# Joint norms between two products: sums gathered beside the first product, the gate factor put on y there, one pass over the tiles after it

## The chip, the cores and the metric

The kernel runs on one core of a Trainium2 chip. The metric is device time in microseconds (us), from the first to the last instruction of one execution; before the change the median of 3 runs is 2791.24 us (2790.05 to 2795.76). TensorE multiplies matrices, VectorE and ScalarE work elementwise, GpSimd too (slower), SyncE issues DMAs. In the profile they are PE (PEld for its weight loads), DVE, ACT, POOL and SP.

## The reference, cut to what matters

The program is a transformer-like block. Two places in it have the same form: a product's output y goes through a norm with gain and gate, is added to the residual x, and the sum goes through a second norm with its modulation into the next product.

```python
def rmsnorm(x, g):
    xf = x.astype(jnp.float32)
    y = xf * lax.rsqrt(jnp.mean(xf * xf, axis=-1, keepdims=True) + EPS)
    return (y * g.astype(jnp.float32)).astype(x.dtype)

def modulate(x, shift, scale):
    return x * (1 + scale) + shift

def half_ffn(h, shift, scale, gate, g_pre, g_post, w13, w2):
    u = modulate(rmsnorm(h, g_pre), shift, scale)
    return h + 0.5 * gate * rmsnorm(swiglu(u, w13, w2), g_post)

new_lat = h_lat + gt_l * rmsnorm(out_l, g_post)     # end of token_mixing
```

Place A: the first half_ffn's w2 product, then the norm in front of w_in. Place B: the token mixing's w_out product, then the norm in front of the second half_ffn. At A 768 tokens are worked on (512 of the sequence and 256 of the context), at B the 512.

## The kernel before, in words

Activations stand feature-major: 128 features on the partitions, tokens along the row, 8 tiles (KT) for 1024 features. So a norm over features sums over tiles and partitions; the sum over partitions is a matmul with a matrix of 1/1024 (mean_ones), which also spreads the mean over all partitions. Every product is done in three passes of fp32r (three_pass, L204 to L206): high part of the weight by high and low part of the data, low part of the weight by the high one. Weights come in slots of up to 128 x 2048 (STREAM): SyncE loads a slot (L169), GpSimd splits it into whi (L186) and wlo (L189) two slots ahead of TensorE, as soon as slot_done says that the buffer is free, and TensorE starts a slot when w_split and acc_free allow (pe_slot_begin). Slots at A: 8 of dn_a1, then gates (1), wk (4) and further ones in project_1. At B: 4 of w_out, then those of gu_b0.

In the last product VectorE adds each tile to y (L843) or copies it (L1833), ScalarE squares it (L526), VectorE adds the square to a running sum (L535). Behind the product stands NormFront: TensorE's mean of the sum (L588), square root on ScalarE in place in PSUM (L605), reciprocal on VectorE (L644) over all tokens; pass one makes y * gain * r and adds x (L637, L665) while ScalarE squares (L620) and TensorE sums (L596); a second root and reciprocal; pass two scales (L637), makes the high part on ScalarE (L628) and the low part on VectorE (L682). The first slot of the next product waits tile by tile for that low part (front.lo_ready); TensorE goes through the slots in order, gates first and then wk. The order of the work on each engine is the order of the code.

## Time and profile before

| | |
|---|---|
| median of 3 runs | 2791.24 us (2790.05 to 2795.76) |
| span of the profiled execution | 2793.2 us (its own time, 2.0 above the median) |
| TensorE busy | 2607.8 us, 93% |
| VectorE, ScalarE, GpSimd busy | 42%, 26%, 48% |

Busy time says what an engine was doing, not what the program waited for; the waits are read in the timelines, where an instruction row ends with the idle time in front of it and what released it. Times count from the span's start. GpSimd's splits of weights show when slots end, since each starts when TensorE has left its buffer.

### The profile page before, as it was taken

The numbers are of one execution on the slowest core, as the hardware profiler recorded it, in microseconds if no ns is written. First come the engines' busy times: TensorE is split into PE (matmuls) and PEld (weight loads), VectorE is DVE, ScalarE is ACT, GpSimd is POOL, SyncE is SP. The second block draws the span as 40 slices with busy tenths as digits, with TensorE's granted clock in tenths as the row PEclk, the third lists the DMA queues.
The fourth block names the chain that finished last, engine by engine and source line by source line (L and its number), as shares of the span: only waits on it lengthen the run. The fifth ranks groups of instructions, "written<-read, shape, count | busy, mean of one in ns | idle before, by whom it ended". The sixth has DMA issues, their size and how long they took to land. (4 is left out here: it accounts for less than half of the span.)

```text
span 2793.2 us, 35776 instructions
## 1 busy us (share of the span) xinstructions
PE 2607.8 (93%) x14270; PEld 2210.2 (79%) x14270; DVE 1172.2 (42%) x1682; ACT 715.5 (26%) x1152; POOL 1353.6 (48%) x431
## 2 busy tenths in 40 slices
PE   6999999995999899998999998999989999969997
PEld 4888888883889788876788886778887898867775
DVE  5112011227476464126310224455426225349997
ACT  5111000102220342101210113334432111126774
POOL 0443455451465035776477775566446777620000
PEclk8999999997999999999999998999999999988999
DMA  7443211112321003232123224220012232439994
GB/s 290 181 184 145 70 62 61 56 64 100 138 76 64 15 19 133 79 109 103 65 87 112 90 88 155 89 85 16 1 54 83 91 122 91 161 152 370 370 375 180
DMA packets 52444, 334.00 MB, mean 120 GB/s; under 512 B 6516, under 2 KB 7540, under 8 KB 19616
## 3 DMA queue, kind: packets, MB, share of 16 engines
q1 hardware_dynamic: 50736, 326.49, 31.5%
q0 software_dynamic: 1584, 5.78, 0.5%
q8 instruction: 87, 1.43, 0.2%
q14 instruction: 37, 0.30, 0.0%
HBM read 313.89 MB, written 22.07 MB: 120 GB/s over the span
## 5 line engine op out<-in xcount | busy, mean ns | idle before, releaser
L186 POOL TENSOR_TENSOR whi<-raw,one_col 128x2048 fp32r<-128x2048 f32 (+2 forms) x158 | 526.0, 3329 | 884.3 <-PE bank L206 782.0
L189 POOL TENSOR_TENSOR wlo<-raw,whi 128x2048 fp32r<-128x2048 f32 (+2 forms) x158 | 697.9, 4417 | 12.4
L204 PE MATMUL bank<-uh_a,whi 128*128 128x512 f32 (+1 forms) x704 | 239.2, 340 | 1.6 <-DVE ul_a L499 1.6
L205 PE MATMUL bank<-ul_a,whi 128*128 128x512 f32 (+1 forms) x704 | 237.5, 337 | 0.0
L206 PE MATMUL bank<-uh_a,wlo 128*128 128x512 f32 (+1 forms) x704 | 237.3, 337 | 0.0
L3383 DVE TENSOR_TENSOR moe_wl<-moe_raw,moe_wh 128x2048 fp32r<-128x2048 f32 x84 | 189.4, 2283 | 7.2 <-DMA xs_scratch<-moe_tok,moe_dest 5.4
L3319 ACT ACTIVATE moe_wh<-moe_raw 128x2048 fp32r<-128x2048 f32 x84 | 159.8, 1912 | 25.1 <-PE bank L3294 19.1
L204 PEld LDWEIGHTS bank<-uh_a,whi 128*128 128x128 f32 x704 | 134.1, 191 | 21.5 <-DVE ul_a L499 3.8
L206 PEld LDWEIGHTS bank<-uh_a,wlo 128*128 128x128 f32 x704 | 134.0, 190 | 14.2
L204 PE MATMUL bank<-uh_b,whi 128*128 128x512 f32 x352 | 138.1, 392 | 7.5 <-DVE ul_b L682 6.5
L205 PEld LDWEIGHTS bank<-ul_a,whi 128*128 128x128 f32 x704 | 134.2, 191 | 13.7
L205 PE MATMUL bank<-ul_b,whi 128*128 128x512 f32 x352 | 137.9, 392 | 0.0
L206 PE MATMUL bank<-uh_b,wlo 128*128 128x512 f32 x352 | 137.7, 391 | 0.0
L3231 POOL DMA_INDIRECT out_dram<-moe_y,moe_rows x7 | 6.7, 950 | 265.0 <-DVE moe_y L3440 265.0
L204 PE MATMUL bank<-fa_hh,whi 128*128 128x512 f32 (+1 forms) x352 | 118.7, 337 | 1.0 <-DVE fa_hl L822 1.0
L205 PE MATMUL bank<-fa_hl,whi 128*128 128x512 f32 (+1 forms) x352 | 118.5, 337 | 0.0
L206 PE MATMUL bank<-fa_hh,wlo 128*128 128x512 f32 (+1 forms) x352 | 118.3, 336 | 0.0
L785 ACT ACTIVATE fa_sil<-bank 128x512 f32<-128x512 f32 x22 | 13.2, 599 | 402.6 <-PE bank L206 402.6
L204 PE MATMUL bank<-xh_r,whi 128*128 128x512 f32 x256 | 100.5, 393 | 5.5 <-POOL wlo L189 3.3
L206 PE MATMUL bank<-xh_r,wlo 128*128 128x512 f32 x256 | 99.7, 389 | 0.0
L205 PE MATMUL bank<-xl_r,whi 128*128 128x512 f32 x256 | 99.6, 389 | 0.0
L3266 PE MATMUL bank<-moe_wh,moe_xsh 128*128 128x512 f32 x224 | 91.4, 408 | 2.9 <-DVE moe_xsl L3389 2.9
(547 smaller groups left out, 6350.0 us busy)
## 6 DMA issues: line engine op xcount, KB each, us to landing
moe_raw<-moe_w_dram SPq DMA_DIRECT2D x84, 1024.0 KB, 7.2
cond_ring<-w_ada_dram SPq DMA_DIRECT2D x27, 1024.0 KB, 6.7
raw<-gu_a_dram SPq DMA_DIRECT2D x22, 1024.0 KB, 5.0
raw<-gu_b_dram SPq DMA_DIRECT2D x22, 1024.0 KB, 4.9
raw<-wqkv_dram SPq DMA_DIRECT2D x12, 1024.0 KB, 4.7
raw<-dn_a_dram SPq DMA_DIRECT2D x16, 704.0 KB, 4.0
raw<-dn_b_dram SPq DMA_DIRECT2D x16, 704.0 KB, 4.0
n_ada<-w_ada_dram SPq DMA_DIRECT2D x9, 1024.0 KB, 19.6
```

The source lines that it names most:

```text
L186: e.nc.gpsimd.tensor_tensor(e.whi[p][:, 0:f], e.raw[p][:, 0:f], e.one_col[:, 0:1].to_broadcast([P, f]), ALU.mult).then_inc(e.w_hi, 1)
L189: e.nc.gpsimd.tensor_tensor(e.wlo[p][:, 0:f], e.raw[p][:, 0:f], e.whi[p][:, 0:f].bitcast(F32), ALU.subtract).then_inc(e.w_split, 1)
L204: e.nc.tensor.matmul(out, wh, xh, start=first, stop=False)
L205: e.nc.tensor.matmul(out, wh, xl, start=False, stop=False)
L206: return e.nc.tensor.matmul(out, wl, xh, start=False, stop=last)
L785: last = nc.scalar.activation(sil[p][:, 0:T], e.bank[2 * p][:, :], ACT.Silu)
L3231: nc.gpsimd.indirect_dma_start(out=e.dram["out"], out_offset=bass.IndirectOffsetOnAxis(ap=rows[r][:, :], axis=0), in_=Y[r][:, :], in_offse ...
L3266: nc.tensor.matmul(out, xsh[b % 2][:, k, :], w[:, cc], start=k == 0, stop=False)
L3319: nc.scalar.activation(wh[s % RING_W][:, :], raw[s % RING_RAW][:, :], ACT.Copy).then_inc(hi_done, 1)
L3383: nc.vector.tensor_tensor(wl[s % RING_W][:, :], raw[s % RING_RAW][:, :], wh[s % RING_W][:, :].bitcast(F32), ALU.subtract).then_inc(lo_done, 1)
```

## The change

NormSums gathers four sums while the product runs: of y squared, of z squared, of x times z and of x squared, where z is y with the gate factor. From the first comes r1, and as the mean of (x + r1 z) squared is xx + 2 r1 xz + r1 r1 zz, the second norm's factor r2 comes from all four without looking at x + r1 z. So the residual x is loaded before the last product and not behind it, ScalarE puts the gate factor on y (gate), and VectorE does five SBUF instructions per tile in the product's slots. For the last tile the gate is left to later, z squared and xz are made with the factor in the instruction. TensorE sums in four strips of tokens, each into 32 partitions of the bank, so that root and reciprocal see 192 or 128 columns instead of 768 or 512; matmuls with pick spread the rows again. JoinedNorm then makes one pass: z = y r1, y = z + x, t = y r2, u = t gs + shift on ScalarE, uh and ul. The first wk slot (at B the second gu_b0 slot) is split by ScalarE and VectorE and skipped by GpSimd. In project_1 first_pair takes gates and the first half of wk's first slot together, tile by tile, then wk's second half. The store of y goes out in eight parts, bias_tok behind it.

```diff
+class NormSums:
...
+    def act(self, act, k, written):
+        nc, r = self.e.nc, k % 2
+        if k == 0:
+            act.wait_ge(*self.x_in)
+        if k >= 2:
+            act.wait_ge(self.summed, max(1, k - 2))
+        nc.scalar.activation(self.tmp["xx"][r][:, :], self.x[:, k, 0:self.w], ACT.Square).then_inc(self.x_squared, 1)
+        if k == KT - 1:
+            nc.scalar.activation(self.e.warm[:, :], self.e.eps[:, 0:1], ACT.Sqrt).then_inc(self.gated, 1)
+        act.wait_ge(*written)
+        nc.scalar.activation(self.tmp["yy"][r][:, :], self.y[:, k, 0:self.w], ACT.Square).then_inc(self.y_squared, 1)
...
+        self.gate(k).then_inc(self.gated, 1)
+        act.wait_ge(self.gated, k + 1)
+        nc.scalar.activation(self.tmp["zz"][r][:, :], self.y[:, k, 0:self.w], ACT.Square).then_inc(self.z_squared, 1)
...
+    def pe(self, pe):
...
+        pe.wait_ge(self.summed, KT - 2)
+        for q in ("xx", "yy", "zz", "xz"):
+            for j in range(NSTRIP):
+                nc.tensor.matmul(self.out(q, j), e.mean_ones[:, 0:32], strips(self.acc[q][:, :])[:, :, 64 * j:64 * j + 64],
+                                 start=True, stop=False)
+        for q in ("xx", "yy", "zz", "xz"):
+            pe.wait_ge(ready[q], KT)
+            for j in range(NSTRIP):
+                last = nc.tensor.matmul(self.out(q, j), e.mean_ones[:, 0:32],
+                                        strips(self.tmp[q][1][:, :])[:, :, 64 * j:64 * j + 64], start=False, stop=True)
+            last.then_inc(self.sum_ready[q], 1)
...
+class JoinedNorm:
...
+    def act(self, act):
...
+        nc.scalar.activation(self.sd1[:, :], e.bank[self.sums.banks["yy"]][:, 0:q], ACT.Sqrt, bias=e.eps[:, 0:1]
+                             ).then_inc(self.sd1_ready, 1)
...
+        nc.scalar.activation(e.whi[p][:, :], e.raw[p][:, :], ACT.Copy).then_inc(e.w_hi, 1)
+        act.wait_ge(self.mean_ready, 1)
+        nc.scalar.activation(self.sd2[:, :], self.d[:, :], ACT.Sqrt, bias=e.eps[:, 0:1]).then_inc(self.sd2_ready, 1)
+        self.unpack(act, self.R1, self.r1, self.r1_psum, self.r1_ready)
...
+        self.unpack(act, self.R2, self.r2, self.r2_psum, self.r2_ready)
...
+    def dve(self, dve):
...
+        dve.wait_ge(self.sd1_ready, 1)
+        V.reciprocal(self.inv1[:, :], self.sd1[:, :]).then_inc(self.inv1_ready, 1)
...
+        link(V.tensor_tensor(self.a[:, :], bank["zz"], self.inv1[:, :], ALU.mult))
+        link(V.scalar_tensor_tensor(self.b[:, :], bank["xz"], 2.0, self.a[:, :], ALU.mult, ALU.add))
+        link(V.tensor_tensor(self.c[:, :], self.b[:, :], self.inv1[:, :], ALU.mult))
+        V.tensor_tensor(self.d[:, :], bank["xx"], self.c[:, :], ALU.add).then_inc(self.mean_ready, 1)
+        dve.wait_ge(self.sd2_ready, 1)
+        V.reciprocal(self.inv2[:, :], self.sd2[:, :]).then_inc(self.inv2_ready, 1)
+        dve.wait_ge(e.w_hi, self.g + 2)
+        V.tensor_tensor(e.wlo[p][:, :], e.raw[p][:, :], e.whi[p][:, :].bitcast(F32), ALU.subtract).then_inc(e.w_split, 1)
...
             feed_sp(e, sp, (fed, sp_span[1]))
             if late_load is not None:
-
-                sp.wait_ge(e.slot_done, START[f"{up}1"][1])
-                sp.dma_start(late_load[0][:, :, :], late_load[1]).then_inc(loaded, 16)
-                sp.wait_ge(loaded, 16)
+                sp.wait_ge(late_load[2], 16)
+                sp.wait_ge(sums.pick_in, 16)
...
-            feed_pool(e, pool, pool_span)
+            feed_pool(e, pool, (pool_span[0] + 1, pool_span[1]))
...
-            slots(pe, *START["gates"], fm(1, True, ready=lambda k: pe.wait_ge(front.lo_ready, k + 1)))
-            slots(pe, *START["wk"], fm(2, True))
+            def first_pair():
...
+                for k in range(KT):
+                    pe.wait_ge(front.lo_ready, k + 1)
+                    at = slice(k * P, (k + 1) * P)
+                    for p in (g % 2, 1 - g % 2):
+                        three_pass(e, e.bank[2 * p][:, :], e.whi[p][:, at], e.wlo[p][:, at], uh[:, k, 0:T], ul[:, k, 0:T],
+                                   k == 0, k == KT - 1)
+                        last = three_pass(e, e.bank[4 + p][:, 0:TC], e.whi[p][:, at], e.wlo[p][:, at], uh[:, k, T:W],
+                                          ul[:, k, T:W], k == 0, k == KT - 1)
+                        if k == KT - 1 and p == g % 2:
+                            last.then_inc(e.slot_done, 1)
```

Three places in the order of the instructions. First VectorE in w_out (place B), before; Y is the product's output, one slot is:

```order
L1833 COPY Y_6989<-bank 128x512
L1833 ISA
L1833 COPY Y_6989<-bank 128x512
L535 TENSOR_TENSOR w_out_run_acc<-w_out_run_acc,w_out_run_sq_6998 128x512 [waits w_out_run_summed,w_out_run_squared]
L530 REGISTER_ALU
L535 TENSOR_TENSOR w_out_run_acc<-w_out_run_acc,w_out_run_sq_6999 128x512 [waits w_out_run_summed,w_out_run_squared]
```

And now, VectorE in the second slot of w_out; XR is x, tmp and acc are NormSums' buffers:

```order
L2118 COPY Y_7318<-bank 128x512 [waits slot_done]
L2118 COPY Y_7318<-bank 128x512
L764 TENSOR_TENSOR s_tmp_xz_7335<-Y_7318,XR_7319 128x512 [waits s3_gated,s3_summed,acc_free]
L775 TENSOR_TENSOR s_acc_yy<-s_acc_yy,s_tmp_yy_7331 128x512 [waits s3_crossed,s3_summed,s3_z_squared,s3_x_squared]
L775 TENSOR_TENSOR s_acc_zz<-s_acc_zz,s_tmp_zz_7333 128x512
L775 TENSOR_TENSOR s_acc_xz<-s_acc_xz,s_tmp_xz_7335 128x512
L775 TENSOR_TENSOR s_acc_xx<-s_acc_xx,s_tmp_xx_7337 128x512
L764 TENSOR_TENSOR s_tmp_xz_7336<-Y_7318,XR_7319 128x512 [waits s3_gated,s3_summed,acc_free]
```

Four more additions follow, then the next slot's copies: ten instructions with two SBUF inputs where two stood. Second, VectorE behind dn_a1 (place A), a tile of pass two before:

```order
L637 SCALAR_TENSOR_TENSOR bank<-y_a,gs,bank 128x512 [waits n2_lo_ready]
L637 SCALAR_TENSOR_TENSOR bank<-y_a,gs,bank 128x256
L682 SCALAR_TENSOR_TENSOR ul_m<-bank,mods,uh_m 128x512 [waits n2_hi_ready]
L682 SCALAR_TENSOR_TENSOR ul_m<-bank,mods,uh_m 128x256
L637 SCALAR_TENSOR_TENSOR bank<-y_a,gs,bank 128x512 [waits n2_lo_ready]
```

And VectorE in the single pass now; n_r1s and n_r2s are the spread factors:

```order
L929 TENSOR_TENSOR y_a<-n_z_3649,xr 128x768 [waits n2_z_ready]
L918 TENSOR_TENSOR n_z_3650<-y_a,n_r1s 128x768 [waits n2_added]
L938 TENSOR_TENSOR n_t_3651<-y_a,n_r2s 128x768 [waits n2_u_ready,n2_added]
L922 TENSOR_TENSOR ul_m<-n_u_3654,uh_m 128x768 [waits n2_hi_ready]
L929 TENSOR_TENSOR y_a<-n_z_3650,xr 128x768 [waits n2_z_ready]
```

The additions of x that stood in pass one are now between the tiles of the only pass. Third, TensorE at the start of the gates slot, before (whi_51 and wlo_53 hold gates):

```order
L204 MATMUL bank<-uh_m,whi_51 128x512 [waits n2_lo_ready,acc_free,w_split]
L205 MATMUL bank<-ul_m,whi_51 128x512
L206 MATMUL bank<-uh_m,wlo_53 128x512
L204 MATMUL bank<-uh_m,whi_51 128x512 [waits n2_lo_ready]
L205 MATMUL bank<-ul_m,whi_51 128x512
```

And TensorE there now (whi_52 and wlo_54 hold wk's first slot):

```order
L204 MATMUL bank<-uh_m,whi_51 128x256
L205 MATMUL bank<-ul_m,whi_51 128x256
L206 MATMUL bank<-uh_m,wlo_53 128x256
L204 MATMUL bank<-uh_m,whi_52 128x512
L205 MATMUL bank<-ul_m,whi_52 128x512
L206 MATMUL bank<-uh_m,wlo_54 128x512
L204 MATMUL bank<-uh_m,whi_52 128x256
L205 MATMUL bank<-ul_m,whi_52 128x256
L206 MATMUL bank<-uh_m,wlo_54 128x256
L204 MATMUL bank<-uh_m,whi_51 128x512 [waits n2_lo_ready]
```

Between two waits for a tile stand twelve matmuls instead of three.

## Rows read from the trace of the kernel before

**Rows 1.** The page, busy time and share of the span by engine:
```profile
PE 2607.8 (93%) x14270; PEld 2210.2 (79%) x14270; DVE 1172.2 (42%) x1682; ACT 715.5 (26%) x1152; POOL 1353.6 (48%) x431
```

**Rows 2.** Busy time by stretches: us; PE, PEld, DVE, ACT, POOL busy; PEclk; DMA; GB/s:
```profile
637.20:680.00 42.80, 16.12 (x36) 7.55 (x36) 33.18 (x46) 13.02 (x18) 8.69 (x2) 0.74 0.23 91
680.00:700.20 20.20, 16.75 (x48) 11.21 (x49) 14.22 (x26) 6.31 (x12) 0.00 (x0) 0.53 0.23 69
1309.50:1339.20 29.70, 11.98 (x18) 3.91 (x19) 22.38 (x26) 10.11 (x15) 8.14 (x2) 0.74 0.17 63
```

**Rows 3.** Timeline of GpSimd, place A: start us, us, engine, line, operation, [idle before]:
```profile
700.48 3.60 POOL L186 TENSOR_TENSOR whi<-raw,one_col 128x2048 fp32r<-128x2048 f32 x1 [54.44 <-PE bank L206]
...
717.14 3.60 POOL L186 TENSOR_TENSOR whi<-raw,one_col 128x2048 fp32r<-128x2048 f32 x1 [8.38 <-PE bank L206]
```

**Rows 4.** Timeline of VectorE, place A:
```profile
616.45 1.25 DVE L535 TENSOR_TENSOR fa_run_acc<-fa_run_acc,fa_run_sq 128x768 f32<-128x768 f32 x1 [1.01 <-ACT fa_run_sq L526]
...
637.33 1.02 DVE L843 TENSOR_TENSOR y_a<-y_a,bank 128x512 f32 x2 [6.28 <-PE bank L206]
...
671.47 4.98 DVE L644 RECIPROCAL bank<-bank 128x512 f32<-128x512 f32 x2 [3.94 <-ACT bank L605]
...
692.12 2.35 DVE L682 SCALAR_TENSOR_TENSOR ul_m<-bank,mods,uh_m 128x512 fp32r<-128x512 f32 x4
```

**Rows 5.** Timeline of TensorE, place A:
```profile
641.74 2.93 PE L588 MATMUL bank<-fa_run_acc,mean_ones 128*128 128x512 f32 x4 [4.55 <-DVE fa_run_acc L535]
...
680.04 0.76 PE L204 MATMUL bank<-uh_m,whi 128*128 128x512 f32 x1 [9.66 <-DVE ul_m L682]
```

**Rows 6.** Timeline of VectorE and ScalarE: the first norm, then place A:
```profile
26.84 7.04 DVE L491 TENSOR_TENSOR n_x<-n_x,n_rstd 128x768 f32<-128x768 f32 x8
...
39.31 2.28 DVE L471 TENSOR_TENSOR wlo<-raw,whi 128x2048 fp32r<-128x2048 f32 x1
...
45.93 1.29 ACT L456 ACTIVATE n_t<-n_x,mods,gs 128x512 f32<-128x512 f32 x2
47.25 0.85 ACT L460 ACTIVATE uh_a<-n_t 128x768 fp32r<-128x768 f32 x1
...
690.02 1.05 ACT L628 ACTIVATE uh_m<-bank,mods 128x512 fp32r<-128x512 f32 x2 [1.18 <-DVE bank L637]
```

**Rows 7.** Timeline of TensorE in the conditioning step (two rows per matmul):
```profile
33.45 1.93 PE L280 MATMUL bank<-n_ada,cond_sc 128*32 128x256 f32 x16 [0.55 <-DMA n_ada<-w_ada_dram]
...
81.44 2.80 PE L280 MATMUL bank<-cond_ring,cond_sc 128*32 128x256 f32 x48
```

**Rows 8.** Groups of instructions by line and shape: busy us, mean ns, idle before:
```profile
L843 DVE TENSOR_TENSOR y_a<-y_a,bank 128x256 f32 x8 | 3.3, 414 | 0.0
```

**Rows 9.** Timeline of TensorE in the first slot of gu_b0:
```profile
1343.63 0.63 PE L205 MATMUL bank<-ul_b,whi 128*128 128x512 f32 x1
...
1344.34 0.40 PE L204 MATMUL bank<-uh_b,whi 128*128 128x512 f32 x1
1344.58 0.40 PE L205 MATMUL bank<-ul_b,whi 128*128 128x512 f32 x1
```

**Rows 10.** Timeline of GpSimd, place B:
```profile
1280.53 4.94 POOL L189 TENSOR_TENSOR wlo<-raw,whi 128x2048 fp32r<-128x2048 f32 x1
...
1320.99 4.54 POOL L189 TENSOR_TENSOR wlo<-raw,whi 128x2048 fp32r<-128x2048 f32 x1
1352.79 3.60 POOL L186 TENSOR_TENSOR whi<-raw,one_col 128x2048 fp32r<-128x2048 f32 x1 [27.26 <-PE bank L206]
```

**Rows 11.** DMA issues: name, queue, count, KB each, us to landing:
```profile
xr<-x_dram SPq DMA_DIRECT2D x1, 3072.0 KB, 11.7
```

**Rows 12.** Timeline of VectorE in w_out:
```profile
1279.38 6.64 DVE L535 TENSOR_TENSOR w_out_run_acc<-w_out_run_acc,w_out_run_sq 128x512 f32<-128x512 f32 x2 [0.80 <-ACT w_out_run_sq L526]
...
1309.58 1.29 DVE L1833 COPY Y<-bank 128x512 f32 x2 [1.74 <-PE bank L206]
1311.69 1.49 DVE L535 TENSOR_TENSOR w_out_run_acc<-w_out_run_acc,w_out_run_sq 128x512 f32<-128x512 f32 x2 [0.81 <-ACT w_out_run_sq L526]
```

More of the change, by code:

```diff
@@ L741, in _ @@
             pool.wait_ge(e.w_split, 2)
-            feed_pool(e, pool, pool_span)
+            feed_pool(e, pool, (pool_span[0] + (front is not None and cond is None), pool_span[1]))
         @block.tensor
@@ L773, in _ @@
                 slots(pe, d0 + 1, d1, down_slot)
+            if sums is not None:
+                sums.pe(pe)
         @block.scalar
@@ L800, in _ @@
                     slots(act, g0, g1, silu_slot)
-            slots(act, *START[f"{down}1"], lambda nm, i, p, g, ih, gh: running.act(act, tile_at(y, i), i, p, g))
+            if sums is None:
+                slots(act, *START[f"{down}1"], lambda nm, i, p, g, ih, gh: running.act(act, tile_at(y, i), i, p, g))
+            else:
+                slots(act, *START[f"{down}1"], lambda nm, i, p, g, ih, gh: sums.act(act, i, (e.acc_free, g + 1)),
+                      straight=True)
         @block.vector
@@ L846, in out_slot @@
                     last.then_inc(e.acc_free, 1)
-                    if half == 1:
+                    if half == 1 and sums is None:
                         running.dve(dve, yv, i, p, g)
-                slots(dve, *START[f"{down}{half}"], out_slot)
+                    elif half == 1:
+                        sums.dve(dve, i, (e.acc_free, g + 1))
+                slots(dve, *START[f"{down}{half}"], out_slot, straight=half == 1 and sums is not None)
     if front is not None:
@@ L999, in tm @@
                 return body
-            slots(pe, *START["gates"], fm(1, True, ready=lambda k: pe.wait_ge(front.lo_ready, k + 1)))
-            slots(pe, *START["wk"], fm(2, True))
+            def first_pair():
+                g = START["gates"][0]
+                pe_slot_begin(e, pe, g)
+                pe_slot_begin(e, pe, g + 1)
+                for k in range(KT):
+                    pe.wait_ge(front.lo_ready, k + 1)
[7 more added lines that the diff above has]
+                            last.then_inc(e.slot_done, 1)
+                p = 1 - g % 2
+                for out, c in ((e.bank[2 * p + 1][:, :], slice(0, T)), (e.bank[4 + p][:, TC:2 * TC], slice(T, W))):
+                    for k in range(KT):
+                        at = slice((KT + k) * P, (KT + k + 1) * P)
+                        last = three_pass(e, out, e.whi[p][:, at], e.wlo[p][:, at], uh[:, k, c], ul[:, k, c], k == 0,
+                                          k == KT - 1)
+                last.then_inc(e.slot_done, 1)
+            first_pair()
+            k0, k1 = START["wk"]
+            slots(pe, k0 + 1, k1, fm(2, True))
             slots(pe, *START["wq"], fm(2, False))
@@ L1015, in _ @@
             act.wait_ge(e.slot_done, g0 + 1)
-            act.wait_ge(front.stored, 16)
+            act.wait_ge(front.stored, 16 * KT)
             nc.scalar.activation(GR[:, 0:T], e.bank[2 * (g0 % 2)][:, :], ACT.Identity, bias=e.params[:, at:at + 1])
@@ L3541, in layout_inputs @@
     dram["strip_sel"] = strip
+    pick = np.zeros((P, NSTRIP, P), np.float32)
+    for m in range(NSTRIP):
+        pick[32 * m, m] = 1.0
+    dram["pick"] = pick.reshape(P, NSTRIP * P)
     def pair(name, wa, wb, w2, half_tiles):
@@ L3696, in program @@
                      product_gate(e, "w_four", 4, yfh, yfl, GF), mixed, out])
+        back_in.close()
     uh, ul = at("uh_b", [P, KT, T], 0, F32R), at("ul_b", [P, KT, T], 16384, F32R)
-    n3 = NormFront(e, "n3", T, Y1, uh, ul, "gu_b0", acc=acc, post=(1, XR), pre=2)
+    n3 = JoinedNorm(e, "n3", sums, uh, ul, 2, START["gu_b0"][0], MAIN + 123904, (e.bank[0],), (e.bank[1],), joint=False)
     Y2 = at("Y2", [P, KT, T], 107520)
```

247 lines of the change are left out of this document (229 added, 18 removed).

## The prediction

> **What bounds the kernel now.** I read first the engines' busy times: TensorE is busy for 93% of a span of 2793.2 us and no other engine, its own weight loads apart, for half of it [rows 1]. A change elsewhere can therefore pay only where TensorE waits, so next I took busy time by stretches around the two places that the diff touches [rows 2]. Place A lies between the last slot of dn_a1 and the first slots of project_1: in the 42.8 us after 637.2 us TensorE works for 16.1, and in the next 20.2 us, the gates slot, its clock is 0.53 of full. Place B lies between w_out and gu_b0: of 29.7 us it works for 12.0, on the norms' own sums. Both waits end with a chain of steps on VectorE and ScalarE.
>
> When a slot ends is best read on GpSimd, which splits the weights two slots ahead as soon as a slot is done. At A gates ends at 700.4 and the first wk slot, wk0, at 717.0 us [rows 3]; dn_a1 ended at 637.2, just before VectorE takes its last tile [rows 4]. My marker is the end of wk0. VectorE at A has two reciprocals of 5.0 us, each with a pass over the tiles behind it; the second pass runs from 676.5 to 694.5 [rows 4]. TensorE gets its first tile at 680.0 us [rows 5], and each of the others waits for its ul_m tile.
>
> **Place A, step by step.** From 637.2 us the last tile is added until 638.35 [rows 4]. ScalarE then squares y (0.85) and squares it again with the gate factor as scale, a pair like the one at 690.02 us, 1.05 us [rows 6]: 640.4. TensorE's sums are eight groups of four matmuls with 32 output rows, 192 columns each. The conditioning step has that shape: 24 matmuls, six groups of 256 columns, took 2.80 us at full clock, 0.47 a group, and two groups 1.93 at half clock [rows 7]. So 0.35 us a group; four fit before 640.4, and the last is done by 641.2. (If the four strips didn't overlap, the groups would cost four times that and A some 7 us more.) Then: square root of 192 columns 0.4 (640.9); reciprocal, 192 columns at 6.5 ns from 4.98 us for 768 [rows 4], 1.3 (642.2); four short dependent steps, each just below the 0.41 us of 256 columns [rows 8] with 0.1 for the semaphore, 1.9 (644.1); square root 0.4 and reciprocal 1.3 (645.9); on VectorE the low part of wk0, 2.28 [rows 6]: 648.3. Its high part, on ScalarE, lies beside the four steps. The spreading matmuls of R1 (768 fp32 columns, 2.93 us [rows 5]) and two unpackings of about 0.5 end before 648.3; those of R2 at about 650, and the first use is at 651.
>
> The pass has four instructions of 768 columns for each tile (z, add, t, low part), all with both inputs in SBUF. Eight such took 7.04 us back to back [rows 6], so 0.87 each, 3.5 us a tile. ScalarE needs 2.1 a tile for u and uh (1.29 and 0.85 [rows 6]) and stays under that. 32 instructions are 28 us; the first add waits for z (0.2) and the last low part for u and uh (about 1.7): 30 us, end at 678.3. The old passes end at 694.5 [rows 4]. So 16 us come from fewer and shorter reciprocals, from joint norms and from one pass.
>
> The other part is first_pair: for each tile TensorE now has gates and the first half of wk0, 12 matmuls, 2.1 us at full clock (0.23 for 512 columns [rows 9] and 0.12 for 256) and 3.8 at half. Of wk0's 16.6 us [rows 3] half has moved under the pass. After 678.3 come 2.1 us for the last tile and 8.3 for the second half: marker at 688.7 against 717.0, **28.3 us gained**. GpSimd's split for wk1 starts when gates is done, 679.4, and takes 3.60 + 4.6 [rows 3, 10]: 687.6, just in time. The cost of a low clock: before, TensorE spent most of the gates slot at half clock, with gaps, and at B, without gaps, it rose after 5 us, at 1344 [rows 2, 9]. Here it has 3.8 us of work per 3.5 at half clock, so it is as dense as at B. If it stays at half clock to the end, the second half costs 16.6 instead of 8.3, +8.
>
> What else moves at A costs nothing by my count. The x load (11.7 us [rows 11]) is issued at 545.4 in front of the load of dn_a1's fourth slot; that one is due on GpSimd at 568.5, 23 us later. The new sums put xz and four additions behind each dn_a1 slot: 1.0 + 5 x 0.87 on VectorE and about 3.6 on ScalarE. VectorE's two-input instructions wait while GpSimd runs (below, at B). So they start after the split, at about 6 us of an 11.46 us slot, and end at 10.7. That just fits, and the last sums are done at 635. The store in eight parts and the bias behind it are waited for by ScalarE's GR (at about 680); the fourth wk load has until 705.
>
> **Place B, where GpSimd's hold on the port that both share decides.** In w_out GpSimd splits 2048 columns (3.60 + 4.6 us) in each of three slots of 10.9 us, and the two additions of a slot took 6.64 us in the first (three such rows), but 1.49 once GpSimd stood still [rows 12]. One gets in between GpSimd's two instructions, the next waits for the end of the second; GpSimd itself waits at most one VectorE instruction (4.94 against 4.54 [rows 10]). New are ten of these per slot instead of two (six in the first). I walk through it with 0.61 us each, between 0.58 (the 0.87 by columns) and 0.75 (half of 1.49, where each waits for the one before): by the end of the second slot (1287.7) xz0, xz1 and two or three additions are done; GpSimd holds the port until 1291.9; one addition; the copy of slot two ends at 1293.9 (about 1289 before), TensorE needs it by 1298.6. In the third window xz2 and two additions by 1299.2, one more at 1302.8, then none until GpSimd is done at 1308. Free from there: six instructions (1311.9), the copy of slot three (1313.1), 1.6 for y squared and the gate on ScalarE, ten (1321.1), the last copy, 1.6, five: 1327.2. Without the lock it would be 1315.7; the old sum was done at 1313.2.
>
> Then at half clock (TensorE idle since 1309.5) eight groups of 0.45, 1330.8, and the block's end, 1331.2 (0.45 from the two groups in 1.93 [rows 7]). Square root, reciprocal (128 columns), four steps, root and reciprocal: 0.4 + 0.9 + 1.8 + 0.5 + 0.9 = 4.5, the low part 2.3: 1338.0. The pass at 512 columns: 0.61 x 4 = 2.4 a tile, 21 in all: 1359.1, and the last six matmuls 1.4: 1360.5. Before, this slot ended at 1352.7 [rows 10]. **7.8 us lost.**
>
> The page "SBUF — State Buffer" of the Trainium skill (Who interferes with whom) speaks against this part: a VectorE instruction with two SBUF inputs and a GpSimd instruction that reads SBUF exclude each other for a whole instruction. The trace agrees (6.64 against 1.49). By a shared bandwidth instead, the additions would only be slower, and B would come out between the two sums.
>
> The sum: 28.3 - 7.8 = 20.5 us, 2793.2 - 20.5 = 2772.7 for an execution like the profiled one. The runs' median, 2791.24, is 2.0 lower: **2770.7 us**. What follows is a sequence bound by TensorE, which moves as a whole; nothing there starts by another clock than the slots.
>
> **The rivals.**
> The lock bites less: VectorE slips in more often and GpSimd, which has 2.3 us of slack a slot, takes the delay. Up to 11.5 us come back at B, 2759. For it: GpSimd's 0.4 more [rows 10] shows that VectorE can pass it. Against: the second addition didn't pass in any of the three windows [rows 12]. 20%.
> Less at A: the clock stays at half behind the pass (+8), or the strips of the sums run in series (+7 at A, +8 at B): 2779 to 2786. For it: 0.53 over the whole gates slot before. Against: the six groups in 2.80 us, and the clock at B [rows 7, 9]. 20%.
> Slower: two-input instructions keep, without GpSimd, the 1.25 us that they show in dn_a1 [rows 4] instead of 0.87, at either width +0.38, on the 64 of both passes and on the 16 that stand alone at the end of w_out: 30 us, 2801. It decides from +0.26 each. Against it speak the 7.04 us for eight and the 1.49 for two; for it only that these rows come from a stage with another layout. 4%.
> The change doesn't do what it says, VectorE's pass is the bound and nothing is won by first_pair (TensorE waits for wk0's split or for a load): +10, 2781, 4%.
>
> **Numbers.** My case has 52%, 2766 to 2776. The range takes in the lock that doesn't bite (2759) with 2 below for its error, and half clock with serial strips at one place: 2757 to 2786. A measurement of this kernel tells 0.2%, 5.6 us, from no change. Faster by more than that, below 2785.6: 92%; within it 4%; slower 4%.
>
> **What would show it.** In the profile after: at A the first uh_m matmul at about 655, then one group of twelve every 3.5 us, the last low part at about 678, wk0's end near 689 (GpSimd's second split after dn_a1). At B the last addition of the sums near 1327 minus the 28 of A, with single additions of 3 to 5 us in w_out, and the first gu_b0 slot longer after w_out than the 43.3 us of before (1309.4 to 1352.7), by about 8. The prediction is wrong if a dn_a1 or w_out slot gets longer (GpSimd would then be the one that waits), if the pass takes over 4 us a tile, or if TensorE is at half clock after the pass.

## The result and the profile after

The changed kernel takes 2770.46 us (median of 4 runs, 2769.15 to 2774.13) against 2791.66 us of the kernel before in the same session (4 runs, 2790.05 to 2795.76): ratio 0.9926, 95% interval 0.9912 to 0.9940. Predicted were 2770.7 us and a range of 2757 to 2786. The profiled execution has a span of 2767.8 us, 25.4 less than the one before.

The page of the profile after, its first row: busy us, share and number of instructions.

```profile
PE 2587.4 (93%) x14376; PEld 2205.1 (80%) x14376; DVE 1205.0 (44%) x1705; ACT 760.8 (27%) x1217; POOL 1334.9 (48%) x427
```

TensorE's busy time is 20 us less than in [rows 1], though its work isn't less: busy time counts clock and stalls too. VectorE and ScalarE have more to do, and the time fell all the same, so totals don't explain it. The stretches do: busy time by stretches, from dn_a1's end to wk0's, in a slot of w_mproj (used below), and from w_out's end to the end of gu_b0's first slot. The columns are those of [rows 2].

```profile
635.90:686.54 50.64, 35.77 (x226) 29.06 (x227) 36.51 (x43) 25.34 (x39) 8.21 (x3) 0.90 0.37 135
...
1188.82:1200.22 11.40, 11.30 (x50) 9.32 (x51) 0.00 (x0) 0.00 (x0) 8.21 (x4) 1.00 0.45 142
...
1276.40:1325.98 49.58, 22.11 (x130) 16.50 (x131) 38.70 (x62) 25.94 (x38) 0.00 (x1) 0.69 0.11 40
```

From the last tile's addition to GpSimd's split behind wk0, A took 79.8 us before (637.33 to 717.14 [rows 3, 4]) and takes 50.6 now: 29.2 gained, 28.3 predicted. B took 43.3 before (from 1309.5, the end of w_out's first slot and three slots of 10.88, to 1352.79 [rows 10]) and takes 49.6: 6.3 lost, 7.8 predicted. Together 22.9. The other 2.5 us between the two spans stand in code that the change doesn't touch: after the change the first split of GpSimd comes 1.3 us earlier, and a slot of w_mproj took 12.98 us before at a clock of 0.87 and 11.40 after at 1.00; the remaining stretches come to 0.4 us the other way. The kernel of A alone (below), which has the same code up to there, has the first split at the old place again and 12.95 us in that slot. So these 2.5 us are differences between executions, and the medians, 21.2 apart, are nearer to the 22.9 than to the 25.4. How finely one execution tells two kernels apart, the traces of all eleven kernels show: the stretch from wk0's end to the end of w_out's first slot took 555.8 to 559.7 us and the stretch behind B 1440.0 to 1445.0, though the kernels do the same work there, while A is 50.6 us in all five kernels that share its code and B 49.5 to 49.6 in five. The intervals can therefore be compared to 0.1 us and whole executions only to a few us. The end of w_out's first slot in the kernel before:

```profile
1276.85 3.60 POOL L186 TENSOR_TENSOR whi<-raw,one_col 128x2048 fp32r<-128x2048 f32 x1 [2.60 <-PE bank L206]
```

GpSimd's splits after the change, the markers of both places (start, us, then the instruction and the idle time ahead of it):

```profile
677.16 3.60 POOL L186 TENSOR_TENSOR whi<-raw,one_col 128x2048 fp32r<-128x2048 f32 x1 [48.19 <-PE bank L206]
...
686.54 3.60 POOL L186 TENSOR_TENSOR whi<-raw,one_col 128x2048 fp32r<-128x2048 f32 x1 [1.10 <-PE bank L206]
...
1243.74 3.60 POOL L186 TENSOR_TENSOR whi<-raw,one_col 128x2048 fp32r<-128x2048 f32 x1 [2.59 <-PE bank L206]
...
1254.62 3.78 POOL L186 TENSOR_TENSOR whi<-raw,one_col 128x2048 fp32r<-128x2048 f32 x1 [2.27 <-PE bank L206]
...
1325.98 3.60 POOL L186 TENSOR_TENSOR whi<-raw,one_col 128x2048 fp32r<-128x2048 f32 x1 [51.42 <-PE bank L206]
```

VectorE at A (it answers to [rows 4]): the last tile, its xz, the first reciprocal, the start of the pass, and its last low part.

```profile
635.93 1.02 DVE L1105 TENSOR_TENSOR y_a<-y_a,bank 128x512 f32<-128x512 f32 x2 [2.38 <-PE bank L206]
636.99 1.15 DVE L760 SCALAR_TENSOR_TENSOR s_tmp_xz<-y_a,gg,xr 128x512 f32<-128x512 f32 x2
639.18 1.35 DVE L899 RECIPROCAL n_inv<-n_sd 128x192 f32<-128x192 f32 x1 [1.04 <-ACT n_sd L860]
...
646.04 0.94 DVE L918 TENSOR_TENSOR n_z<-y_a,n_r1s 128x768 f32<-128x768 f32 x1
647.02 0.96 DVE L929 TENSOR_TENSOR y_a<-n_z,xr 128x768 f32<-128x768 f32 x1
647.89 0.95 DVE L918 TENSOR_TENSOR n_z<-y_a,n_r1s 128x768 f32<-128x768 f32 x1
...
674.67 0.96 DVE L922 TENSOR_TENSOR ul_m<-n_u,uh_m 128x768 fp32r<-128x768 f32 x1 [1.38 <-ACT uh_m L885]
```

The whole chain from the last tile to the first z takes 10.1 us, as much as two reciprocals alone took before (5.0 each [rows 4]); two-input instructions of the pass follow each other by 0.87 us (647.02, 647.89), as the prediction took them.

TensorE at A (it answers to [rows 5]): the sums in strips (first, second and last group), the spreading of the first factor, and the first matmuls of two tiles.

```profile
635.82 0.53 PE L784 MATMUL bank<-s_acc_xx,mean_ones 128*32 128x192 f32 x8
636.17 0.51 PE L784 MATMUL bank<-s_acc_yy,mean_ones 128*32 128x192 f32 x8
...
639.24 0.51 PE L789 MATMUL bank<-s_tmp_xz,mean_ones 128*32 128x192 f32 x8
640.67 1.54 PE L830 MATMUL bank<-n_inv,s_pick 128*128 128x192 f32 x8 [0.93 <-DVE n_inv L899]
...
653.34 0.76 PE L204 MATMUL bank<-uh_m,whi 128*128 128x512 f32 x1 [7.74 <-DVE ul_m L922]
...
667.14 0.50 PE L204 MATMUL bank<-uh_m,whi 128*128 128x512 f32 x1 [1.12 <-DVE ul_m L922]
```

Groups of twelve matmuls start at 663.67, 667.14 and 670.62, 3.48 us apart, and each waits about 1.1 us for its low part: VectorE is the bound. The last two tiles come faster, since z has already been made for them (673.35 and 675.69, with waits of 0.4 and 0.0). The clock by stretches of the same place:

```profile
653.30:658.80 5.50, 5.46 (x16) 4.62 (x17) 5.50 (x7) 3.35 (x5) 0.00 (x0) 0.50 0.20 76
658.80:675.60 16.80, 13.11 (x69) 10.61 (x68) 15.38 (x18) 10.77 (x15) 0.00 (x0) 1.00 0.19 70
```

It is 0.50 for the first 5.5 us, in which TensorE has no gap, and 1.00 from then on, with TensorE at work for 78%.

VectorE in w_out and behind it, where the lock was predicted (it answers to [rows 12]):

```profile
1254.25 0.69 DVE L775 TENSOR_TENSOR s_acc_xz<-s_tmp_xz,s_tmp_xz 128x512 f32<-128x512 f32 x1
1254.85 4.09 DVE L775 TENSOR_TENSOR s_acc_xx<-s_tmp_xx,s_tmp_xx 128x512 f32<-128x512 f32 x1
...
1270.02 5.09 DVE L764 TENSOR_TENSOR s_tmp_xz<-Y,XR 128x512 f32<-128x512 f32 x1
...
1277.73 1.28 DVE L2118 COPY Y<-bank 128x512 f32<-128x512 f32 x2
...
1292.71 0.68 DVE L775 TENSOR_TENSOR s_acc_xx<-s_acc_xx,s_tmp_xx 128x512 f32<-128x512 f32 x1
1293.31 0.74 DVE L760 SCALAR_TENSOR_TENSOR s_tmp_xz<-Y,gg,XR 128x512 f32<-128x512 f32 x1
```

An addition or an xz takes 0.6 us where GpSimd stands still, 4.09 and 5.09 where it is at work: 1254.85 is held until GpSimd's high part (1254.62, 3.78) is done, and 1270.02 until the low part is (from 1269.62, 4.94). The copy of the third slot starts at 1277.73, 12.2 us after that slot's end, and the last addition of the sums ends at 1293.4, 17.0 us behind w_out.

### The profile page after: what moved, and what is told of

Its sections match the earlier page's. It is cut to its first block and busy times, and to the rows that moved or that the text cites. A ratio compares the mean times of both kernels' runs of the same rounds, so it can differ in the third digit from the quotient of the medians.

```text
span 2767.8 us, 36011 instructions
## 1 busy us (share of the span) xinstructions
PE 2587.4 (93%) x14376; PEld 2205.1 (80%) x14376; DVE 1205.0 (44%) x1705; ACT 760.8 (27%) x1217; POOL 1334.9 (48%) x427
## 5 line engine op out<-in xcount | busy, mean ns | idle before, releaser
L186 POOL TENSOR_TENSOR whi<-raw,one_col 128x2048 fp32r<-128x2048 f32 (+2 forms) x156 | 520.4, 3336 | 876.7 <-PE bank L206 782.6
L189 POOL TENSOR_TENSOR wlo<-raw,whi 128x2048 fp32r<-128x2048 f32 (+2 forms) x156 | 684.8, 4390 | 12.2
```

The costliest lines, as they stand in the source:

```text
L186: e.nc.gpsimd.tensor_tensor(e.whi[p][:, 0:f], e.raw[p][:, 0:f], e.one_col[:, 0:1].to_broadcast([P, f]), ALU.mult).then_inc(e.w_hi, 1)
L189: e.nc.gpsimd.tensor_tensor(e.wlo[p][:, 0:f], e.raw[p][:, 0:f], e.whi[p][:, 0:f].bitcast(F32), ALU.subtract).then_inc(e.w_split, 1)
```

## The experiments

Intervals are read as above: A from VectorE's last addition to y in dn_a1 to GpSimd's split behind wk0, B from w_out's end (its first slot's end and three slots of 10.88) to the end of gu_b0's first slot. Where GpSimd makes no split in w_out, its end is that of TensorE's last matmul, which in the changed kernel is 0.1 us earlier than the other reading. Before they are 79.8 and 43.3, after 50.6 and 49.6 us.

### w_out_split: GpSimd out of w_out

```diff
-            feed_pool(e, pool, pool_span)
+            feed_pool(e, pool, (pool_span[0], pool_span[1] - (3 if runs[-1].seg == "w_out" else 0)))
...
     def act_body(act, i, p, g):          # in product_out_sums
+        if i < 3:
+            act.wait_ge(e.w_landed[p], 16 * ((g + 2) // 2) + 16)
+            act.wait_ge(e.slot_done, g + 1)
+            act.wait_ge(e.w_split, g + 2)
+            e.nc.scalar.activation(e.whi[p][:, :], e.raw[p][:, :], ACT.Copy).then_inc(e.w_hi, 1)
...
         last.then_inc(e.acc_free, 1)     # in dve_body, behind the copies
+        if i < 3:
+            dve.wait_ge(e.w_hi, g + 3)
+            e.nc.vector.tensor_tensor(e.wlo[p][:, :], e.raw[p][:, :], e.whi[p][:, :].bitcast(F32), ALU.subtract
+                                      ).then_inc(e.w_split, 1)
```

> The changed kernel, but GpSimd is left out of w_out too: the three weight splits that it makes there (w_out[2], w_out[3], gu_b0[0]; 3.6 + 4.9 us each) are made by ScalarE (high part, 1.90 us) and VectorE (low part, 2.28 us), each behind its copy out of the accumulator. My theory: in the changed kernel the sums at B end 17.0 us after w_out because GpSimd holds the port against VectorE's two-input instructions. VectorE's own work in a slot is 1.2 (copies) + 2.3 + 10 x 0.61 = 9.6 of 10.9 us, so it keeps up here, and after w_out only the copies, ScalarE's y squared and gate, and about ten instructions are left: sums end 5 to 7 us after w_out, the interval from w_out's end to the end of gu_b0[0] falls from 49.5 to about 39, and the time from 2770.5 to about 2760. Rival 1: the delay is VectorE's amount of work, not the port: 6.8 us more work on it makes the sums end later, the interval is 50 to 56, the time 2771 to 2777. Rival 2: the split now comes too late for TensorE in w_out, slots grow from 10.88 us, and the gain is lost there: within 3 us of 2770.

Measured: 2757.73 us (4 runs, 2757.30 to 2761.86), ratio to the kernel before 0.9879, interval 0.9861 to 0.9896. VectorE at the end of w_out, GpSimd's splits around B, and TensorE's first and last group of sums:

```profile
1268.42 2.29 DVE L2127 TENSOR_TENSOR wlo<-raw,whi 128x2048 fp32r<-128x2048 f32 x1 [0.71 <-ACT whi L2113]
1270.63 0.68 DVE L764 TENSOR_TENSOR s_tmp_xz<-Y,XR 128x512 f32<-128x512 f32 x1
...
1282.84 0.68 DVE L775 TENSOR_TENSOR s_acc_xx<-s_acc_xx,s_tmp_xx 128x512 f32<-128x512 f32 x1
1283.44 0.74 DVE L760 SCALAR_TENSOR_TENSOR s_tmp_xz<-Y,gg,XR 128x512 f32<-128x512 f32 x1
```

```profile
1233.89 3.60 POOL L186 TENSOR_TENSOR whi<-raw,one_col 128x2048 fp32r<-128x2048 f32 x1 [2.60 <-PE bank L206]
...
1316.10 3.60 POOL L186 TENSOR_TENSOR whi<-raw,one_col 128x2048 fp32r<-128x2048 f32 x1 [73.92 <-PE bank L206]
```

```profile
1283.58 0.66 PE L784 MATMUL bank<-s_acc_xx,mean_ones 128*32 128x128 f32 x8 [6.32 <-DVE s_acc_xx L775]
...
1286.57 0.65 PE L789 MATMUL bank<-s_tmp_xz,mean_ones 128*32 128x128 f32 x8
```

VectorE has three instructions of 2.29 us more to do (one at 1268.42) and is done 10.8 us sooner: the last addition of the sums ends 6.2 us behind w_out (1277.3 to 1283.5) instead of 17.0. xz, which took 1.3 to 5.1 us beside GpSimd, takes 0.68. B falls by the same 10.8 us, from 49.6 to 38.8, and the time from 2770.5 to 2757.7; the 1.9 us by which the time fell further lie outside B and are of the size by which executions differ. So the delay was the port and not the amount of work, rival 1 is excluded, and the slots kept their 10.88 us, which excludes rival 2. This kernel beats both: with GpSimd out of w_out the new scheme gains 4.5 us at B, where it lost 6.3 (the old scheme wasn't run without GpSimd).

### a_only: the old scheme at B

```diff
-            feed_pool(e, pool, (pool_span[0] + (front is not None and cond is None), pool_span[1]))
+            feed_pool(e, pool, pool_span)
...
-        out = product_out_sums(e, "w_out", yh, yl, Y1, res_in, XR, dram["h1"], START["w_four"][1], sums, mixed_ready)
+        out, acc = product_out(e, "w_out", yh, yl, Y1, XR, dram["h1"], START["w_four"][1], True, mixed_ready)
...
-    n3 = JoinedNorm(e, "n3", sums, uh, ul, 2, START["gu_b0"][0], MAIN + 123904, (e.bank[0],), (e.bank[1],), joint=False)
+    n3 = NormFront(e, "n3", T, Y1, uh, ul, "gu_b0", acc=acc, post=(1, XR), pre=2)
```

> The changed kernel with the new scheme at A alone: w_out, its running sum, the norm n3 and GpSimd's split of gu_b0[1] are as in the kernel before. By the two traces the change gave 29 us at A and took 6.2 at B (49.5 against 43.3 us from w_out's end to gu_b0[0]'s end). Theory: the two places are independent, since all behind B moves as a whole: B's interval is 43.3 again and the time 2764 (2762 to 2767). Rival: part of B's loss is given back further on (loads or the experts start at times of their own), so that taking it away gives less: 2767 to 2771, with the interval at 43.3 but a smaller lead at the end.

Measured: 2763.96 us (4 runs, 2762.12 to 2766.82), ratio 0.9895, interval 0.9878 to 0.9912. GpSimd's splits:

```profile
1244.76 3.60 POOL L186 TENSOR_TENSOR whi<-raw,one_col 128x2048 fp32r<-128x2048 f32 x1 [2.60 <-PE bank L206]
...
1320.67 3.60 POOL L186 TENSOR_TENSOR whi<-raw,one_col 128x2048 fp32r<-128x2048 f32 x1 [27.25 <-PE bank L206]
```

w_out ends at 1277.4 (1244.76 and three slots of 10.88), and gu_b0's first slot at 1320.67: 43.3 us as before. All of B's loss comes back, and the median falls by as much, 2770.5 less 6.5: further on nothing of it is given away, as far as the scatter of the runs lets one see. The two places are independent.

### pool_a and pool_b: GpSimd back for the split ahead

The edit takes ScalarE's high part and VectorE's low part of the second slot out of JoinedNorm, at A or at B, and gives that slot to feed_pool again. Shown are the lines as they leave the one place; in the kernels they stand behind a condition, so that the other place keeps them.

```diff
...
-        nc.scalar.activation(e.whi[p][:, :], e.raw[p][:, :], ACT.Copy).then_inc(e.w_hi, 1)
...
-        V.tensor_tensor(e.wlo[p][:, :], e.raw[p][:, :], e.whi[p][:, :].bitcast(F32), ALU.subtract).then_inc(e.w_split, 1)
...
-            feed_pool(e, pool, (pool_span[0] + 1, pool_span[1]))     # pool_a; pool_b the same in ffn
+            feed_pool(e, pool, pool_span)
```

> The changed kernel with GpSimd back at A: it splits wk0 as soon as dn_a1 is done (3.60 + 4.5 us, over about 8.2 us later), in place of ScalarE's 1.90 and VectorE's 2.23. Theory (GpSimd's hold on the port that it shares with VectorE): the last tile's xz, two VectorE instructions with both inputs in SBUF, 1.1 us in the changed kernel, get in only between GpSimd's two instructions and behind them: xz done about 8 us after dn_a1 instead of 2.9, everything behind it 5 to 6 us later, less the 2.2 us of the low part that is gone from VectorE: 3 to 4 us lost, wk0's end 53.5 to 55 us after dn_a1 instead of 50.6, time about 2774. Rival (no hold, or it is hidden by the steps on 192 columns): VectorE only saves its 2.2 us: 48.4 us, time 2768.

Measured: 2776.23 us (4 runs, 2771.43 to 2777.70), ratio 0.9937, interval 0.9918 to 0.9955. GpSimd's split behind wk0 is shown first and, in the second block, VectorE at A:

```profile
691.61 3.60 POOL L186 TENSOR_TENSOR whi<-raw,one_col 128x2048 fp32r<-128x2048 f32 x1 [1.09 <-PE bank L206]
```

```profile
638.16 7.77 DVE L760 SCALAR_TENSOR_TENSOR s_tmp_xz<-y_a,gg,xr 128x512 f32<-128x512 f32 x2
...
651.18 0.96 DVE L920 TENSOR_TENSOR n_z<-y_a,n_r1s 128x768 f32<-128x768 f32 x1 [0.54 <-ACT n_r1s L852]
```

The two xz instructions take 7.77 us together instead of 1.15. The first z stands 14.1 us behind the last addition (637.11 to 651.18) instead of 10.1, and A takes 54.5 us: 3.9 more, as the theory had it; the median rose by 5.8 us, with runs from 2771.4 to 2777.7. The page "SBUF — State Buffer" of the Trainium skill (Who interferes with whom) calls it an exclusive lock for the length of an instruction; the trace agrees, with 7.77 against 1.15 us.

> The changed kernel with GpSimd back at B: it splits gu_b0[1] as soon as w_out is done (8.2 us), in place of ScalarE and of VectorE's 2.23 us. In the changed kernel about 14 of VectorE's two-input instructions are still to come at that point. Theory (the port): two of them get in before and between GpSimd's two instructions, the others wait: the sums end about 7 us later than the 17.0 after w_out, less the 2.2 of the low part: interval 54 to 56 instead of 49.5, time 2775 to 2777. Rival (no hold): 2.2 us gained, 47.3, time 2768.

Measured: 2774.51 us (4 runs, 2773.74 to 2775.11), ratio 0.9941, interval 0.9925 to 0.9958; B takes 54.9 us. GpSimd and the addition and the z of VectorE that it holds at B:

```profile
1302.04 3.60 POOL L186 TENSOR_TENSOR whi<-raw,one_col 128x2048 fp32r<-128x2048 f32 x1 [27.32 <-issue]
...
1331.50 3.60 POOL L186 TENSOR_TENSOR whi<-raw,one_col 128x2048 fp32r<-128x2048 f32 x1 [20.96 <-PE bank L206]
```

```profile
1302.23 3.96 DVE L931 TENSOR_TENSOR Y<-n_z,XR 128x512 f32<-128x512 f32 x1
1306.11 4.98 DVE L920 TENSOR_TENSOR n_z<-Y,n_r1s 128x512 f32<-128x512 f32 x1
```

The number fits the theory (54 to 56), but the way to it doesn't. GpSimd doesn't split when w_out is done: gu_b0 stands in the next block of the program, and ScalarE takes up the next block's first root at 1297.56, only when TensorE's last sum of w_out (1296.58, 0.65 us) is done. GpSimd comes 4.5 us later still. In the code the clearing of the stages' semaphores stands on GpSimd between the blocks; that this takes the 4.5 us is likely, but no run shows it. So GpSimd idles for 27.3 us, comes in at 1302.04, when the pass begins (1301.56), and holds two of its first instructions (3.96 and 4.98 us instead of 0.6); the last addition ends at 1293.5, 17.0 us behind w_out as in the changed kernel. The kernel before shows the same in its own way: GpSimd's split there stands at 1317.3, behind its sum's end at 1313.2. I had not seen that.

### no_pair, no_pair_tiles, no_pair_filled: what first_pair is worth

```diff
-            first_pair()
-            k0, k1 = START["wk"]
-            slots(pe, k0 + 1, k1, fm(2, True))
+            slots(pe, *START["gates"], fm(1, True, ready=lambda k: pe.wait_ge(front.lo_ready, k + 1)))
+            slots(pe, *START["wk"], fm(2, True))
```

> The changed kernel without first_pair: TensorE takes all tiles of the gates slot as they come (6 matmuls a tile) and then wk0 with both halves. The pass on VectorE is the bound (3.48 us a tile) and does not change. Theory: gates ends about 1 us behind the last low part, wk0's 16.6 us follow whole: the interval from dn_a1's end to wk0's end grows from 50.6 to 58, time 2778. Rival 1 (clock): with 1.05 us of work in 3.48 TensorE falls to its lower clock under the pass, and wk0 begins at half clock: 3 to 8 us more, 61 to 66 us, time 2781 to 2786. Rival 2: first_pair brings nothing, since TensorE waits for the pass either way: 50.6 us and 2770.

Measured: 2782.42 us (7 runs, 2781.42 to 2786.41), ratio 0.9967, interval 0.9955 to 0.9980; A takes 62.0 us (637.5 to 699.53), 11.4 more. By its number that is the clock rival, but TensorE's rows show two causes: the old order of the slot takes the 256-column matmuls of all tiles, 24 of them, behind the last tile. TensorE, and then GpSimd's split behind wk0:

```profile
678.70 0.41 PE L204 MATMUL bank<-uh_m,whi 128*128 128x256 f32 x1
...
682.44 0.28 PE L206 MATMUL bank<-uh_m,wlo 128*128 128x256 f32 x1
682.56 0.40 PE L204 MATMUL bank<-uh_m,whi 128*128 128x512 f32 x1
```

```profile
699.53 3.60 POOL L186 TENSOR_TENSOR whi<-raw,one_col 128x2048 fp32r<-128x2048 f32 x1 [8.38 <-PE bank L206]
```

They run from 678.70 to 682.56, where wk0 begins, at first 0.21 us apart (half clock), at the end 0.12 (full). Two more kernels separate the causes. In both a function of the following form stands in the place of first_pair; no_pair_tiles has q = p alone and so takes the six matmuls of gates with each tile, no_pair_filled adds six more, whose result is not used, for each of the first seven tiles.

```diff
-            first_pair()
-            k0, k1 = START["wk"]
-            slots(pe, k0 + 1, k1, fm(2, True))
...
+                for k in range(KT):
+                    pe.wait_ge(front.lo_ready, k + 1)
+                    at = slice(k * P, (k + 1) * P)
+                    for q in (p, 1 - p) if k < KT - 1 else (p,):     # no_pair_tiles: for q in (p,):
+                        three_pass(e, e.bank[2 * q][:, :], e.whi[p][:, at], e.wlo[p][:, at], uh[:, k, 0:T], ul[:, k, 0:T],
+                                   k == 0 or q != p, k == KT - 1 or q != p)
+                        last = three_pass(e, e.bank[4 + q][:, 0:TC], e.whi[p][:, at], e.wlo[p][:, at], uh[:, k, T:W],
+                                          ul[:, k, T:W], k == 0 or q != p, k == KT - 1 or q != p)
+                last.then_inc(e.slot_done, 1)
...
+            slots(pe, *START["wk"], fm(2, True))
```

> As no_pair, but TensorE takes all 6 matmuls of a tile of the gates slot when the tile comes (no_pair left the 256-column ones, 24 of them, behind the last tile: gates ended 5.7 us after the last low part). TensorE has 1.05 us of work in 3.48 at full clock, 2.1 at half. Theory (the clock is one part of what first_pair brings): the clock stays at half under the pass, gates ends about 2.1 us after the last low part and wk0, 16.6 at full clock, begins at half: wk0 ends 20 to 22 us after the last low part, 60 to 61.5 after dn_a1. Rival (the clock rises on its own): 1.05 + 16.6: 57.5.

> As no_pair_tiles, but behind the 6 matmuls of each of the first seven tiles come 6 more of the same shape whose result is not used, so that TensorE is as densely filled as with first_pair, though nothing of wk0 is done. Theory: the clock rises to full during the pass as in the changed kernel, gates ends 1.1 us after the last low part, wk0 follows at full clock: 17.7 us after the last low part, 57 to 58 after dn_a1; against the 50.6 of the changed kernel the 7 left over are the half of wk0 that isn't moved under the pass. Rival (the clock of no_pair has another cause than the gaps): like no_pair_tiles, 60 to 61.5.

One profiled run each: 2781.86 and 2779.57 us. Busy time by stretches under the pass (columns as in [rows 2]), no_pair_tiles and then no_pair_filled, each with its GpSimd split behind wk0:

```profile
665.00:675.00 10.00, 7.18 (x19) 5.43 (x20) 9.57 (x11) 6.76 (x10) 0.00 (x0) 0.50 0.21 79
```

```profile
695.56 3.60 POOL L186 TENSOR_TENSOR whi<-raw,one_col 128x2048 fp32r<-128x2048 f32 x1 [8.38 <-PE bank L206]
```

```profile
665.00:675.00 10.00, 7.17 (x37) 5.76 (x37) 9.83 (x12) 6.79 (x11) 0.00 (x0) 1.00 0.21 79
```

```profile
695.39 3.60 POOL L186 TENSOR_TENSOR whi<-raw,one_col 128x2048 fp32r<-128x2048 f32 x1 [8.38 <-PE bank L206]
```

The clock did what the theory said: 0.50 while TensorE has one slot's work in the gaps of the pass, 1.00 where it is filled. But it is worth little: A is 58.3 and 57.9 us (from 637.25 and 637.51). With VectorE as the bound, half clock only shows behind the last tile, where gates ended 1.95 us after the last low part in the one and 1.5 in the other, with wk0's 16.66 us at full clock behind it in both. It is that little because the clock of no_pair_tiles rose in time, at about 677.6, within the last tile's matmuls; had it risen later, wk0 would have begun at half clock. I had expected just that, 60 to 61.5 for no_pair_tiles, which is wrong. What first_pair gives is so: 7.3 us for what of wk0 lies under the pass (57.9 to 50.6), 3.7 for the 256-column matmuls that no longer stand behind the last tile (62.0 to 58.3), and 0.4 for the clock. Some 0.9 of the 3.7 is clock too, since the first ten of the 24 matmuls in no_pair stand 0.21 us apart instead of 0.12. The whole times don't show the 3.7: 2782.42 for no_pair and 2781.86 for the one run of no_pair_tiles, whose stretches outside A and B are some 4 us longer, within what the same work was seen to differ by. These shares rest on the intervals alone.

### keep_clock: TensorE kept at work while the sums end

```diff
+        if self.st.name == "s3":       # in NormSums.pe, on top of w_out_split
+            g = START["w_out"][1] - 1
+            pe.wait_ge(e.acc_free, g)
+            pe.wait_ge(self.pick_in, 16)
+            for _ in range(7):
+                nc.tensor.matmul(e.bank[2 * (1 - g % 2)][:, :], e.mean_ones[:, :], self.pick[:, :], start=True, stop=True)
```

> The kernel w_out_split with seven added matmuls (fp32, 512 columns, their result is not used) on TensorE behind w_out's last slot, so that it doesn't stand idle while VectorE and ScalarE finish the sums (6.8 us in w_out_split). Theory: after that idle time TensorE's clock is at half, and the eight groups of the sums (0.43 us each) lie on the chain; kept at full clock they take about 0.25, the interval from w_out's end to gu_b0[0]'s end falls from 38.8 to 37.3, time 2756. Rival 1: the added work runs past the end of the sums (7 x 0.85 = 6.0 us at full clock, but 12 at half) and delays them: 40 or more, 2759 or more. Rival 2: the clock of the groups is half anyway: 38.8, 2757.7.

Measured: 2758.87 us (4 runs, 2757.19 to 2759.13), ratio 0.9883, interval 0.9866 to 0.9899. TensorE's first and last group of sums:

```profile
1285.55 0.43 PE L790 MATMUL bank<-s_acc_xx,mean_ones 128*32 128x128 f32 x8 [0.31 <-DVE s_acc_xx L775]
...
1287.10 0.40 PE L795 MATMUL bank<-s_tmp_xz,mean_ones 128*32 128x128 f32 x8
```

The groups stand 0.22 us apart instead of 0.43 (1283.58 to 1286.57 above), and B takes 37.2 us, 1.6 less, as expected. The time doesn't show it: 2756 was expected, and 2758.87 against 2757.73 lies within what the runs scatter. The mechanism and its 1.6 us in B are shown, a gain in the time isn't.

### no_warm: the table of the square root

```diff
-            nc.scalar.activation(self.e.warm[:, :], self.e.eps[:, 0:1], ACT.Sqrt).then_inc(self.gated, 1)
```

> The changed kernel without the one-element square root that ScalarE computes ahead of the last tile's squares at both places. My prediction counted 0.4 us for the square root behind the sums and nothing for the load of its table, 1.28 us in the profile after, which that one element draws forward to 629.2, into ScalarE's idle time. Theory: without it the load stands right ahead of the first square root, behind the last square, on the chain at both places: 1.3 us each, the intervals grow from 50.6 to 51.9 and from 49.5 to 50.8, time 2773. Rival: ScalarE loads the table while TensorE still makes the sums, where it waits anyway: at A (0.3 us between the last square and the root) that hides little, at B (4 us of sums) all of it: 1.3 at A, nothing at B, time 2772.

Measured: 2772.78 us (4 runs, 2769.01 to 2774.00), ratio 0.9924, interval 0.9906 to 0.9942. ScalarE at A and at B:

```profile
640.21 1.28 ACT L860 ACT_TABLE_LOAD   x1
...
1301.44 1.28 ACT L860 ACT_TABLE_LOAD   x1 [5.22 <-PEq L121]
```

A takes 52.0 us and B 50.9, 1.4 and 1.3 more. At B the load stands at the start of the next block, behind the sums (1301.44, where ScalarE had been idle for 5.2 us), as the theory had it; the rival, for which it would hide there, is wrong. The medians (2772.8 and 2770.5, ranges that overlap) agree without proving it. The page "ScalarE: Activation LUTs" of the Trainium skill (What ACT_TABLE_LOAD costs) gives about 1283 ns for the load, which the row shows, and about 1380 ns more for a drain. The drain isn't seen here: at A from the end of the last square to the root are 1.3 us.

## Why the prediction was right

**What bounds.** TensorE's waits at A and B were the place to look: they make 22.9 us, and the medians are 21.2 apart.

**A, the chain.** From the last tile's addition to the first z 11.0 us were predicted (637.3 to 648.3) and 10.1 measured. The groups of the sums stand 0.35 us apart, as taken from [rows 7] (635.82 and 636.17): the four strips run beside each other, and the rival of serial strips is excluded. The reciprocals took 1.35 us (1.3 predicted), the four steps 0.39 each (0.48). The spreading took 1.54 us and not 2.93: TensorE had hardly stood still and its clock was full (1.00 from 637 to 646; in pool_a, after 5.4 us of idle time and at a clock of 0.50, the same four matmuls, eight rows, took 2.90). It was off the chain, and nothing came of it. The table of the square root, which the prediction didn't count, was drawn forward; left in its place it costs 1.4 us.

**A, the pass.** 30 us predicted, 29.6 measured (646.04 to 675.63), at 0.87 us an instruction. The slower rival, two-input instructions at 1.25 us, is excluded by the same rows. Leaving GpSimd out belongs to the chain in front of the pass: pool_a lost 4.0 us there (14.1 instead of 10.1). From the last tile's addition to the last low part the chain and the pass took 57.1 us before and take 39.7 now, 17.4 less, where 16 were predicted. Of these 7.3 are the reciprocals (10.0 us before, 2.7 now, and on the chain both times); how the rest divides between the joint norms, the single pass and the split that GpSimd gave up, no run separates, pool_a's 4 us apart.

**A, first_pair.** Some 12 of the 28.3 us were laid to it (28.3 less the 16 of the pass); taking it out cost 11.4. The prediction named half of wk0, 8.3, but the last tile's share of that half, 1.0, isn't hidden, and its own sum has it so: 2.1 and 8.3 us behind the last low part instead of 1.05 and 16.6 are 7.3 less, as measured. The rest isn't the clock in the main but the 256-column matmuls, which the prediction had in its count of before and didn't name. The clock rose under the pass after 5.5 us, as at B before, and the rival of half clock behind the pass (+8) did not come.

**A, edits costed at nothing.** The slots of dn_a1 stayed at 11.46 us, and the last additions ended at 633.5, 2.4 us before dn_a1's end: it just fits, as worked out. xz waits there for GpSimd too (3.52 and 2.12 us in the last two slots), at no cost. The x load, the store in parts and the late bias left no wait in A's interval.

**B.** The sums ended 17.0 us behind w_out, 17.8 predicted; w_out_split shows by undoing it that it is the lock. From there to the end of the slot 32.6 us against 33.3. The walk through the windows holds nearly step by step. It had two or three additions in the gap ahead of the second split, and three got in (1253.04 to 1254.25); it had two in the third window, and three got in there too (1264.19 to 1265.40), so that the third slot's copy ended at 1279.0 where the walk, moved by the 33.1 us by which w_out starts earlier, had 1280.0. The rival in which the lock bites less (2759) is not what this kernel does, but it is, to 2 us, what the kernel takes once GpSimd is gone from w_out.

**The sum.** 29.2 - 6.3 = 22.9 measured, 28.3 - 7.8 = 20.5 predicted; both terms were a little pessimistic. That the time itself, 2770.46, lies 0.2 us from the 2770.7 is therefore in part luck: the 2.4 us that the two places gained beyond the sum show only by 0.7 in the medians, whose distance is 21.2. None of the signs named beforehand for a wrong prediction came: no slot of dn_a1 or w_out got longer by more than 0.1 us, the pass took 3.5 us a tile, and the clock was full behind it.

## What to carry to other kernels

Before work goes to VectorE beside a GpSimd that splits weights, count how many of its instructions read two operands from SBUF and how long GpSimd leaves the port free in a slot: here ten such instructions of 0.6 us a slot ended 11 us late, and giving 6.9 us more work to VectorE to get GpSimd out of the way made the kernel 12.7 us faster, of which 10.8 are seen at their place. A change that does the same thing at two places is to be timed at each of them by a marker of its own; here 29 us gained hid 6 lost. Where one engine paces another tile by tile, move into its gaps everything that needs only the tiles at hand, the small matmuls as well.
